# A chunked recurrence scan whose rounds get finer steps, a split product and a kept output bank

## The chip, the cores and the metric

The kernel runs on one NeuronCore of a Trainium2 chip. The metric is the device time of one execution in microseconds (us). The engines are TensorE (PE; its weight loads are PEld), VectorE (DVE), ScalarE (ACT), GpSimd (POOL) and SyncE (SP), each with an in-order queue of its own; they meet only through semaphores.

## The reference, cut to what matters

The reference is two transformer blocks on 256 tokens and 256 context tokens. The change touches one part of the second block, the RWKV scan of its first layer: for 8 heads of 64 and two directions, a state S of 64x64 is carried over 512 tokens.

```python
def step(S, inp):
    r_t, w_t, k_t, v_t, a_t, b_t = inp
    sa = jnp.einsum('bhij,bhj->bhi', S, a_t)
    S = (S * w_t[:, :, None, :] + sa[..., None] * b_t[:, :, None, :]
         + v_t[..., None] * k_t[:, :, None, :])
    return S, jnp.einsum('bhij,bhj->bhi', S, r_t)
s_fin, ys = lax.scan(step, state0, xs, reverse=reverse)
```

## The kernel before, in words

**Units.** The 512 tokens are cut into 4 chunks of 128. A unit is one chunk of one direction d and one pair of heads j (two heads fill the 128 partitions): 4 steps x 4 pairs x 2 directions = 32 units (`self.todo`), numbered n. The eight units of one step are independent of each other; unit n continues the state of unit n-8. The units use four sets of buffers in turn (`self.sets`, NS = 4), so unit n takes over the tiles of unit n-4.

**What a unit does.** ACT makes exponentials of the cumulated decay (EB, EI, three single columns in sm). DVE makes from them RA (two 128x128 parts) and KB (two parts, KB0 and KB1), and scales the state ("ts"). PE multiplies each part of KB with RA, for each of the two heads hh: this is the "four matrices' product" mm, 128x512 for each head, in two PSUM banks. DVE copies it through a triangular mask into MM (`copy_predicated`, two copies of 128x512), which POOL has set to zero before (`memset` of 128x1024). PE transposes KB (kbt), ACT copies that to KBt. ACT copies the diagonal blocks of MM to MC.

Then I plus the strict triangle is inverted in seven levels, i = 0 to 6, of block size 1, 2, ... 64. For level i, POOL makes ML_i, the product of MC with that level's mask (i = 0 to 5; "ml"). PE makes lev_i from ML_i and the factors XX, ACT copies it to T1 ("t"), PE makes xx_i from T1 and XX, and DVE adds it to the factors ("x"; x5 goes to XF in three operations, x6 is one copy). ML is one tile, so ML_1 waits until XX's start has read ML_0; XX shares its tile with KB, so XX's start waits for the transposes. The last level uses XF and MM.

wu0 (PE, 6 records in the trace: state and MM times RA and v) is copied by ACT to WU0; wu1 (PE) gives u, which ACT copies to WU1. st (PE) is KBt times u and KBt times v; y (PE) is state times RA, and MM times u and v. DVE copies or adds y to the output tile and adds st to the state. y of unit n-4 frees the buffers for unit n.

**Order.** The order on every engine is written out by hand. `run` goes through rounds r = 0 to 178; a unit starts every five rounds (APART = 5), and in each round every running unit, oldest first, executes its code up to the next `yield`. So unit n is at its own round r-5n, and four units run at the same time. On PE a unit's own rounds are: 3 mm and kbt, 5 lev0, 6 lev1, 7 xx1, 8 lev2, ... 15 xx5, 16 lev6 and wu0, 17 xx6, 18 wu1, 19 st and y. On POOL: 1 the memset, 3+2i the product ML_i. At the end of a round `close` (steps of the output norm of head pairs 0 to 3, from rounds 146, 159, 165 and 175 on) and `beside` (the output projection of the attention, f = 5, 6, 7 in rounds 0, 2, 4, the bonus term in rounds 4 to 14, the router in round 149) are put in.

**Banks.** `Banks.take` hands out the eight PSUM banks in turn; a taker waits for the tokens of the one before in that bank, which `done` has set.

Helper lines in the profile: L144 matmul, L147 transpose, L150 ACT activation, L153 tensor_tensor, L158 tensor_scalar, L161 scalar_tensor_tensor, L164 tensor_copy, L173 copy_predicated, L179 memset. A matmul has two records in the trace ("x8" is four matmuls). Names: the tiles of set 0 lie in `rwa`; MC and ML lie in rwWU, KB in rwXX, EI in rwT, T1 of set 3 in nv; ps is a PSUM bank.

Of the kernel before, what the change touches and what calls it, by code (L numbers as in the profile page):

```python
# [9 lines left out]
U32 = mybir.dt.uint32  # L10
# [2423 lines left out]
class Rwkv:  # L2434
# [112 lines left out]
    def pe(self, e, beside, amid):  # L2547
# [29 lines left out]
        S.meet(e, p, "prep")  # L2577
        self.run(e, self.unit_pe, self.close_pe, amid)
        S.meet(e, p)
# [93 lines left out]

    def run(self, e, unit, close=None, beside=None):


        running, closing = [], []
        for r in range(self.CLOSE[-1] + 4):
# [6 lines left out]
            assert len(running) <= self.NS  # L2685
# [5 lines left out]
            if beside is not None:  # L2691
                beside(e, r)

# [87 lines left out]
    def unit_pe(self, e, n, step, d, j, B):  # L2781
# [6 lines left out]
        yield  # L2788
        yield
        yield  # L2790
        got = []
        for hh in range(2):
            got.append(g.banks.take(("mm", n, hh)))
            for tok in g.banks.free(("mm", n, hh)):
                e.wait_ge(*tok)
        e.wait_ge(*S.dve.at(("kb", n)))
        for q in range(2):
            for hh, b in enumerate(both):
                ins = e.matmul(got[hh][:, q * 256:(q + 1) * 256], KB[b, q, :], RA[b, :], True, True)
                if q:  # L2800
                    ins.then_inc(*p.up(("mm", n, hh)))
        ps = g.banks.take(("kbt", n))
        for tok in g.banks.free(("kbt", n)):
            e.wait_ge(*tok)
        for q in range(2):
            ins = e.transpose(ps[:, q * P:(q + 1) * P], KB[:, q, :], g.C("ident"))
        ins.then_inc(*p.up(("kbt", n)))
        yield
        for i, li in self.levels():
            yield  # L2810
# [16 lines left out]
            if li == 0:  # L2827
                self.wu0_pe(e, n, RA, MM, state, v)
            if i:
                yield  # L2830
# [16 lines left out]
        yield  # L2847
# [8 lines left out]
        yield  # L2856
        u = WU[:, 1, :]
        e.wait_ge(*S.act.at(("wu1", n)))
        if step < 3:
            ps = g.banks.take(("st", n))  # L2860
            for tok in g.banks.free(("st", n)):
                e.wait_ge(*tok)
            e.wait_ge(*S.act.at(("kbt", n)))
            e.matmul(ps[:, 0:P], KBt[:, 0, :], u, True, False)
            e.matmul(ps[:, 0:P], KBt[:, 1, :], v, False, True).then_inc(*p.up(("st", n)))
        ps = g.banks.take(("y", n))
        for tok in g.banks.free(("y", n)):
            e.wait_ge(*tok)
        e.matmul(ps[:, 0:P], state, RA[:, P:2 * P], True, False)
        for hh, b in enumerate(both):  # L2870
            e.matmul(ps[b, 0:P], u[:, b], MM[:, hh, 128:256], False, False)
        for hh, b in enumerate(both):
            ins = e.matmul(ps[b, 0:P], v[:, b], MM[:, hh, 384:512], False, True)
        ins.then_inc(*p.up(("y", n)))

    def wu0_pe(self, e, n, RA, MM, state, v):
# [4 lines left out]
        e.wait_ge(*S.dve.at(("ts", n)))  # L2881
        e.matmul(ps[:, 0:P], RA[:, 0:P], state, True, False)
# [4 lines left out]
    def unit_act(self, e, n, step, d, j, B):  # L2887
# [7 lines left out]
        yield  # L2895
        if n >= self.NS:
            e.wait_ge(*S.pe.at(("y", n - self.NS)))
            e.wait_ge(*S.dve.at(("end", n - self.NS)))
        e.activation(sm[:, 0:1], mc, ACT.Copy, scale=self.DECAY).then_inc(*a.up())
        e.activation(sm[:, 2:3], mc, ACT.Copy, scale=-self.DECAY).then_inc(*a.up())  # L2900
        e.wait_ge(*a.now())
        e.activation(EB[:, e0:e0 + P], cu, ACT.Exp, scale=-self.DECAY, bias=sm[:, 0:1]).then_inc(*a.up())
        e.activation(EI[:, :], cu, ACT.Exp, scale=self.DECAY, bias=sm[:, 2:3]).then_inc(*a.up())
        e.activation(sm[:, 1:2], mc, ACT.Exp, scale=-self.DECAY).then_inc(*a.up())
        x0 = 0 if d == 0 else 128
        e.activation(EB[:, x0:x0 + 1], mc, ACT.Exp, scale=self.DECAY).then_inc(*a.up(("eb", n)))
        yield
        yield
        e.wait_ge(*S.dve.at(("mk", n)))
        for b in (slice(0, 64), slice(64, 128)):  # L2910
            e.activation(B["MC"][b, :, :], B["MM"][b, :, b], ACT.Copy).then_inc(*a.up(("mc", n)))
        e.wait_ge(*S.pe.at(("kbt", n)))
        e.activation(KBt[:, :, :], two(g.banks.of(("kbt", n))[:, 0:256]), ACT.Copy).then_inc(*a.up(("kbt", n)))
        g.banks.done(("kbt", n), a.now())
        yield
        for i, li in self.levels():
            yield
            if i:
                e.wait_ge(*S.pe.at(("t", n, i)))
                rows = slice(0, P) if li else dst  # L2920
                e.activation(T1[rows, :, :], two(g.banks.of(("lev", n, i))[rows, 0:128]), ACT.Copy).then_inc(*a.up(("t", n, i)))
                g.banks.done(("lev", n, i), a.now())
                if li == 0:
                    e.wait_ge(*S.pe.at(("wu0", n)))
                    e.activation(WU[:, 0, :], g.banks.of(("wu0", n))[:, 0:P], ACT.Copy).then_inc(*a.up(("wu0", n)))
                    g.banks.done(("wu0", n), a.now())
                yield
        yield
# [3 lines left out]
        yield  # L2932

    def unit_dve(self, e, n, step, d, j, B):
# [7 lines left out]
        yield  # L2942
        yield
# [5 lines left out]
        e.tensor_tensor(KB[:, 0, :], self.BB[d][:, j, cc], EI[:, :], MUL).then_inc(*v.up())  # L2949
        e.tensor_tensor(KB[:, 1, :], self.KD[d][:, j, cc], EI[:, :], MUL).then_inc(*v.up(("kb", n)))  # L2950
        e.wait_ge(*v.now())
        e.tensor_scalar(state, state, sm[:, 1:2], None, MUL).then_inc(*v.up(("ts", n)))
        yield
        mask = mid(g.C(f"tri{d}").bitcast(U32), 2, 256)
        for hh in range(2):
            e.wait_ge(*S.pe.at(("mm", n, hh)))
            e.wait_ge(*S.pool.at(("mz", n)))
            e.copy_predicated(two(MM[:, hh, :]), mask, two(g.banks.of(("mm", n, hh))[:, :])).then_inc(*v.up(("mk", n)))
            g.banks.done(("mm", n, hh), v.now())
        yield  # L2960
        for i, li in self.levels():
            yield
            if i == 0:
                one = mid(self.IC[:, :], 2, 64)
                e.wait_ge(*S.pool.at(("ml", n, 0)))
                e.wait_ge(*S.act.at(("kbt", n)))
                e.tensor_tensor(XX[:, 1, :, :], ML[:, :, :], one, ADD).then_inc(*v.up())
                e.wait_ge(*S.pe.at(("t", n, 0)))
                e.tensor_tensor(XX[:, 0, :, :], two(g.banks.of(("lev", n, 0))[:, 0:128]), one, ADD).then_inc(*v.up(("x", n, 0)))
                g.banks.done(("lev", n, 0), v.now())  # L2970
            else:
                yield
                ps = g.banks.of(("xx", n, i))
                e.wait_ge(*S.pe.at(("x", n, i)))
                e.wait_ge(*v.at(("x", n, i - 1)))
                if li > 1:
                    xx = XX[:, :, :, :].rearrange("p q h n -> p (q h n)")
                    e.tensor_tensor(xx, xx, ps[:, 0:256], ADD).then_inc(*v.up(("x", n, i)))
                elif li:
                    x0 = XX[:, 0, :, :].rearrange("p h n -> p (h n)")  # L2980
                    e.tensor_tensor(x0, x0, ps[:, 0:128], ADD).then_inc(*v.up())
                    e.wait_ge(*S.pool.at("compact"))
                    for b in (slice(0, 64), slice(64, 128)):
                        e.tensor_tensor(XF[b, :, b], XX[b, 1, :, :], two(ps[b, 128:256]), ADD).then_inc(*v.up(("x", n, i)))
                else:
                    e.tensor_copy(XF[src, :, dst], two(ps[src, 0:128])).then_inc(*v.up(("x", n, i)))
                g.banks.done(("xx", n, i), v.now())
        yield
        yield
# [8 lines left out]
        if step < 3:  # L2998
            last = e0 + (P - 1 if d == 0 else 0)
            e.wait_ge(*S.pe.at(("st", n)))  # L3000
            e.wait_ge(*v.at(("ts", n)))
            for lo in (0, 64):
                q = slice(lo, lo + 64)
                e.tensor_tensor(state[q, q], state[q, q], g.banks.of(("st", n))[q, q], ADD).then_inc(*v.up())
            g.banks.done(("st", n), v.now())
            e.wait_ge(*v.now())
            e.tensor_scalar(state, state, EB[:, last:last + 1], None, MUL).then_inc(*v.up())
        v.note(("end", n))

    def unit_pool(self, e, n, step, d, j, B):  # L3010
        g, o, S = self.g, self.S.pool, self.S
# [1257 lines left out]
```

## Time and profile before

| what | value |
|---|---|
| median of 3 runs | 2538.28 us (2536.87 to 2542.72) |
| the profiled execution | 2542.52 us, its span 2540.7 us |
| PE busy | 2341.8 us, 92% |
| DVE, ACT, POOL busy | 69%, 41%, 13% |
| one unit of the scan in the steady part | 10.1 us |

The span is the time between the first and the last instruction in the profile; the execution has some us around it. In the table of busy time the groups that cost most belong to other stages; the scan lies between about 1405 and 1757 us. In the rows of the timeline, a line gives start, duration, engine, line, operation, the tiles written and read, shapes and count, and in brackets the idle time of this engine before it and who ended that.

### The profile page before, as it was taken

How to read it: one execution, taken by the hardware profiler on the slowest of the kernel's cores; microseconds unless marked ns; L12 is line 12 of the kernel's file. 1: busy time of each engine (PE TensorE's matmuls, PEld its weight loads, DVE VectorE, ACT ScalarE, POOL GpSimd, SP SyncE). 2: the span in 40 equal slices, each digit the busy share in tenths (PEclk: the TensorE clock that was granted, in tenths of full speed). 3: DMA queues.
4: the chain of work that ended last, by engine and by line, in shares of the span. 5: the costliest groups of instructions: out<-in, count | busy, mean ns of one | idle time of the engine just before them, and what ended most of it. 6: DMA issues, size and time to landing. Idle time of an engine off the chain costs nothing.

```text
span 2540.7 us, 38727 instructions
## 1 busy us (share of the span) xinstructions
PE 2341.8 (92%) x15014; PEld 1751.2 (69%) x15014; DVE 1744.4 (69%) x3348; ACT 1051.7 (41%) x2068; POOL 337.2 (13%) x534
## 2 busy tenths in 40 slices
PE   7999999799989799989999899989999998998997
PEld 3788887465788799944454677775676775667775
DVE  4875687677756687834758666665678885748995
ACT  4222212224231434423134344442477773446884
POOL 0111110010001011000200233331011210001210
PEclk9999999899999899989998999999899999999998
DMA  8566654242226478711111000000389982126995
GB/s 307 190 204 199 216 197 161 94 141 91 101 74 206 142 265 269 254 43 66 39 43 35 18 3 3 2 3 26 109 286 341 324 314 108 59 70 216 338 339 188
DMA packets 114919, 386.47 MB, mean 152 GB/s; under 512 B 20144, under 2 KB 22320, under 8 KB 114480
## 3 DMA queue, kind: packets, MB, share of 16 engines
q1 hardware_dynamic: 76496, 275.81, 31.2%
q0 software_dynamic: 34848, 95.47, 11.3%
q10 hardware_dynamic: 3392, 12.72, 1.3%
q8 instruction: 119, 1.95, 0.3%
q14 instruction: 64, 0.52, 0.1%
HBM read 389.16 MB, written 26.21 MB: 163 GB/s over the span
## 4 chain that ended last, share of the span: by engine, by line
PE 37%; DVE 13%; DMA 8%; ACT 5%; issue 3%; POOL 0%; DVEq 0%; ACTq 0%; SPq 0%; POOLq 0%
PE ps L144 35%; DMA RG<-in_w 5%; DVE moe0wl L153 2%; PE ps L147 2%; DVE moe1wl L153 2%; DMA AR<-in_a 2%; DVE rwMM L173 1%; DVE f2wl L153 1%; DVE acc L161 1%; ACT moe0wh L150 1%; DVE H L161 1%; ACT moe1wh L150 1%; DVE rwXF L153 1%; ACT rwWU L150 1%; DVE rwXX L153 0%
## 5 line engine op out<-in xcount | busy, mean ns | idle before, releaser
L144 PE MATMUL ps<-H,RG 128*128 128x256 f32 (+2 forms) x1088 | 359.4, 491 | 14.0 <-ACT H L150 14.0
L161 DVE SCALAR_TENSOR_TENSOR acc<-AR,cs,acc 128x512 f32<-128x512 f32 x420 | 295.5, 746 | 48.9 <-DMA AR<-in_a 46.7
L144 PEld LDWEIGHTS ps<-H,RG 128*128 128x128 f32 (+1 forms) x1088 | 206.1, 194 | 149.8 <-issue 132.5
L153 DVE TENSOR_TENSOR moe0wl<-RG,moe0wh 128x1024 fp32r<-128x1024 f32 x144 | 173.6, 1219 | 42.8 <-ACT moe0wh L150 33.1
L150 ACT ACTIVATE moe0wh<-RG 128x1024 fp32r<-128x1024 f32 x144 | 150.8, 1061 | 73.9 <-DMA RG<-in_w 44.5
L200 POOL DMA_DIRECT2D AR<-in_a x152 | 82.1, 540 | 698.8 <-DVE acc L161 512.5
L150 ACT ACTIVATE f1wh<-RG 128x1024 fp32r<-128x1024 f32 x66 | 69.7, 1060 | 230.0 <-PE ps L144 229.9
L153 DVE TENSOR_TENSOR moe1wl<-RG,moe1wh 128x1024 fp32r<-128x1024 f32 x120 | 144.2, 1219 | 23.9 <-ACT moe1wh L150 19.8
L144 PE MATMUL ps<-f1hh,f1wh 128*128 128x512 f32 x352 | 142.5, 405 | 4.8 <-DVE f1hl L153 4.8
L150 ACT ACTIVATE moe1wh<-RG 128x1024 fp32r<-128x1024 f32 x120 | 125.9, 1060 | 46.8 <-DMA RG<-in_w 28.4
L144 PE MATMUL ps<-f1hl,f1wh 128*128 128x512 f32 x352 | 140.8, 400 | 0.0
L144 PE MATMUL ps<-f1hh,f1wl 128*128 128x512 f32 x352 | 140.7, 400 | 0.0
L153 DVE TENSOR_TENSOR f1wl<-RG,f1wh 128x1024 fp32r<-128x1024 f32 x66 | 80.4, 1221 | 54.8 <-ACT f1wh L150 53.1
L144 PE MATMUL ps<-f2hh,f2wh 128*128 128x256 f32 x352 | 103.2, 293 | 9.7 <-DVE f2hl L153 5.0
L144 PE MATMUL ps<-f2hh,f2wl 128*128 128x256 f32 x352 | 101.5, 288 | 0.0
L144 PE MATMUL ps<-f2hl,f2wh 128*128 128x256 f32 x352 | 101.4, 288 | 0.0
L150 ACT ACTIVATE f2wh<-RG 128x1024 fp32r<-128x1024 f32 x66 | 68.5, 1055 | 47.9 <-PE ps L144 47.9
L144 PE MATMUL ps<-moe0wh,moe0xh 128*128 128x512 f32 x184 | 78.6, 427 | 9.4 <-DVE moe0wl L153 9.3
L153 DVE TENSOR_TENSOR rwXX<-rwXX,ps 128x256 f32<-128x256 f32 (+1 forms) x120 | 47.1, 393 | 58.1 <-PE ps L144 57.5
L144 PE MATMUL ps<-rwa 64*64 64x64 f32 (+3 forms) x1228 | 74.5, 236 | 12.1 <-DVE rwa L153 5.6
L153 DVE TENSOR_TENSOR f2wl<-RG,f2wh 128x1024 fp32r<-128x1024 f32 x66 | 80.3, 1219 | 7.8 <-ACT f2wh L150 7.7
L144 PEld LDWEIGHTS ps<-f1hh,f1wh 128*128 128x128 f32 x352 | 68.6, 195 | 20.4 <-DVE f1hl L153 6.2
(633 smaller groups left out, 5742.3 us busy)
## 6 DMA issues: line engine op xcount, KB each, us to landing
RG<-in_w SPq DMA_DIRECT2D x524, 512.0 KB
AR<-in_a POOLq DMA_DIRECT2D x152, 512.0 KB, 3.9
moe0back<-moe_outs ACTq DMA_DIRECT2D x4, 1024.0 KB, 8.0
CT<-in_consts ACTq DMA_DIRECT2D x1, 2562.0 KB, 14.9
X<-in_x ACTq DMA_DIRECT2D x1, 2048.0 KB, 11.5
moe_rows<-moe0ht POOLq DMA_DIRECT2D x4, 512.0 KB, 5.4
moe1back<-moe_outs ACTq DMA_DIRECT2D x2, 1024.0 KB, 5.8
X<-in_ctx ACTq DMA_DIRECT2D x1, 1024.0 KB, 5.8
```

The lines of the kernel that those rows point to most:

```text
L144: return Silent() if self.e is None else self.e.matmul(out, lhs, rhs, start=start, stop=stop, skip_group_check=True)
L147: return Silent() if self.e is None else self.e.transpose(out, x, ident)
L150: return Silent() if self.e is None else self.e.activation(out, x, f, **k)
L153: return Silent() if self.e is None else self.e.tensor_tensor(out, a, b, op)
L161: return Silent() if self.e is None else self.e.scalar_tensor_tensor(out=out, in0=a, scalar=s, in1=b, op0=op0, op1=op1)
L173: return Silent() if self.e is None else self.e.copy_predicated(out, mask, data)
L200: return Silent() if self.e is None else self.e.dma_start(out, src)
```

## The change

- `run` passes over the running units four times in a round (`SLOTS = 4`, slots 0 to 3), and each unit's code says for every piece in which of its rounds and which slot it stands (`to(r, slot)`); within a slot the oldest unit is first.
- mm is made and masked in halves. PE multiplies KB0 with RA in the unit's round 2, slot 2, and KB1 with RA in round 3, slot 2, each into a bank per head of which 256 columns are used (four banks per unit in place of two); DVE masks them at 3.0 and 4.2 in four copies of 128x256. RA and KB0 are made at 2.1, KB1 at 3.0.
- The transposes move from behind mm to behind lev0 (5.2), ACT's copy of them to 5.2.
- wu0 stands before lev6 (16.0 and 16.1) instead of behind it.
- y and the state's product share PSUM bank 7, which is kept for them; the other seven turn. State times RA, and KBt times v, come at 17.3, before wu1 (18.0); the parts with u, and MM times v, at 19.2.
- DVE updates the state at 20.0 and takes y at 21.0 (step 3, which has no update: y at 20.0).
- ACT makes the columns and EI at 0.0, waiting for xx6 and ts of unit n-4, and EB at 1.0, waiting for the end of unit n-4.
- POOL's memset of MM goes to 0.0 (it waits for y of unit n-4, as before), ML_0 to 4.1, ML_i to (4+2i).1.

The core of the diff:

```diff
-        b = self.n % len(self.tiles)
-        self.n += 1
+        b = self.n % self.turning if kept is None else kept
+        self.n += kept is None
...
+        g.banks.turning = 7
         self.run(e, self.unit_pe, self.close_pe, amid)
+        g.banks.turning = 8
...
-            for u in list(running):
-                if next(u, "over") == "over":
-                    running.remove(u)
+            for _ in range(self.SLOTS):
+                for u in list(running):
+                    if next(u, "over") == "over":
+                        running.remove(u)
...
+    def clock(self):
+        at = [0]
+        def to(r, slot):
+            for _ in range(r * self.SLOTS + slot - at[0]):
+                at[0] += 1
+                yield
+        return to
...
# unit_pe
+        yield from to(2, 2)
+        self.mm_pe(e, n, 0, KB, RA)
+        yield from to(3, 2)
+        self.mm_pe(e, n, 1, KB, RA)
         for i, li in self.levels():
+            r = 4 + 2 * i if i else 5
+            if i == 6:
+                yield from to(r, 0)
+                self.wu0_pe(e, n, RA, MM, state, v)
+            yield from to(r, 1)
...
+            if i == 0:
+                yield from to(r, 2)
+                ps = g.banks.take(("kbt", n))
...
+            else:
+                yield from to(r + 1, 1)
                 key = ("xx", n, i)
...
+        yield from to(17, 3)
+        out = g.banks.take(("y", n), 7)
...
+        e.matmul(out[:, 0:P], state, RA[:, P:2 * P], True, False)
+        if step < 3:
+            e.wait_ge(*S.act.at(("kbt", n)))
+            e.matmul(out[:, P:2 * P], KBt[:, 1, :], v, False, False)
+        yield from to(18, 0)
         ps = g.banks.take(("wu1", n))
...
+        yield from to(19, 2)
...
+            e.matmul(out[:, P:2 * P], KBt[:, 0, :], u, False, True).then_inc(*p.up(("st", n)))
...
+    def mm_pe(self, e, n, q, KB, RA):
+        g, p, S = self.g, self.S.pe, self.S
+        got = []
+        for hh in range(2):
+            got.append(g.banks.take(("mm", n, q, hh)))
+            for tok in g.banks.free(("mm", n, q, hh)):
                 e.wait_ge(*tok)
+        e.wait_ge(*S.dve.at(("kb", n, q)))
+        for hh, b in enumerate((slice(0, 64), slice(64, 128))):
+            e.matmul(got[hh][:, 0:256], KB[b, q, :], RA[b, :], True, True).then_inc(*p.up(("mm", n, q, hh)))
...
# unit_dve
+        def masks(q):
+            for hh in range(2):
+                e.wait_ge(*S.pe.at(("mm", n, q, hh)))
+                e.wait_ge(*S.pool.at(("mz", n)))
+                e.copy_predicated(MM[:, hh, q * 256:(q + 1) * 256], mask,
+                                  g.banks.of(("mm", n, q, hh))[:, 0:256]).then_inc(*v.up(("mk", n, q)))
...
# unit_pool
-        yield
+        to = self.clock()
+        yield from to(0, 0)
         if n >= self.NS:
             e.wait_ge(*S.pe.at(("y", n - self.NS)))
         e.memset(MM[:, :, :], 0.0).then_inc(*o.up(("mz", n)))
-        yield
         for i, li in self.levels()[:-1]:
-            yield
+            yield from to(4 + 2 * i if i else 4, 1)
             if i:
-                yield
                 e.wait_ge(*S.pe.at(("t", n, i - 1)))
                 e.wait_ge(*S.dve.at(("x", n, 0)))
```

## Rows read from the trace of the kernel before

**Rows 1.** The page, busy time by engine.
```profile
span 2540.7 us, 38727 instructions
...
PE 2341.8 (92%) x15014; PEld 1751.2 (69%) x15014; DVE 1744.4 (69%) x3348; ACT 1051.7 (41%) x2068; POOL 337.2 (13%) x534
```

**Rows 2.** The chain of waits over the scan: start, length, what.
```profile
1439.37 0.71 PE ps L144 x16
...
1568.25 1.34 DVE rwa L173 x2
...
1692.24 0.71 PE ps L144 x16
```

**Rows 3.** Timeline of PE over one period: lev6 to the next xx5.
```profile
1562.35 0.44 PE L144 MATMUL ps<-rwXX,rwMM 64*64 64x64 f32 x4 [0.36 <-DVE rwXF L153]
1562.72 0.49 PE L144 MATMUL ps<-rwst,rwRA 128*128 128x128 f32 x2
...
1563.54 0.45 PE L144 MATMUL ps<-rwXX,rwT 64*64 64x64 f32 x8
...
1564.74 0.45 PE L144 MATMUL ps<-rwXX,rwWU 64*64 64x64 f32 x8 [0.24 <-DVE rwXX L153]
...
1565.59 0.66 PE L144 MATMUL ps<-rwWU,rwXF 128*128 128x64 f32 x4
1566.22 0.45 PE L144 MATMUL ps<-rwXX,rwT 64*64 64x64 f32 x8
...
1567.06 1.13 PE L144 MATMUL ps<-rwa 64*128 64x256 f32 x8
1568.13 0.44 PE L147 MATMUL ps<-CT,rwa 128*128 128x128 f32 x2
...
1569.43 0.39 PE L144 MATMUL ps<-rwMM,rwvk 128*64 128x128 f32 x4
1569.75 0.45 PE L144 MATMUL ps<-rwXX,rwWU 64*64 64x64 f32 x8
...
1570.88 0.45 PE L144 MATMUL ps<-rwXX,rwT 64*64 64x64 f32 x8 [0.21 <-ACT rwT L150]
```

**Rows 4.** Timeline of POOL in that period.
```profile
1563.89 0.95 POOL L179 MEMSET rwa<- 128x1024 f32 x1
1564.80 0.46 POOL L153 TENSOR_TENSOR rwWU<-rwWU,nv 128x128 f32<-128x128 f32 x1
1565.28 0.46 POOL L153 TENSOR_TENSOR rwWU<-rwWU,rwa 128x128 f32<-128x128 f32 x1
```

**Rows 5.** Timeline of DVE: the copy of x6.
```profile
1564.72 0.29 DVE L164 COPY rwXF<-ps 64x128 f32<-64x128 f32 x1
```

**Rows 6.** Timelines of DVE and POOL, 1414 to 1419 us.
```profile
1414.96 0.75 DVE L161 SCALAR_TENSOR_TENSOR rwk<-rwk,VT,abr 128x512 f32<-128x512 f32 x1
...
1418.36 0.94 DVE L161 SCALAR_TENSOR_TENSOR rwk<-rwk,VT,abr 128x512 f32<-128x512 f32 x1
...
1418.30 0.45 POOL L153 TENSOR_TENSOR rwWU<-rwWU,nv 128x128 f32<-128x128 f32 x1 [5.74 <-ACT rwWU L150]
1418.71 0.90 POOL L153 TENSOR_TENSOR rwa<-rwa 128x128 f32<-128x128 f32 x1
```

**Rows 7.** Timelines of DVE and PE at the scan's start.
```profile
1401.23 0.88 DVE L161 SCALAR_TENSOR_TENSOR X<-ps,AC,X 128x256 f32<-128x256 f32 x2 [5.99 <-PE ps L144]
...
1402.22 0.28 DVE L153 TENSOR_TENSOR rwa<-abr,rwa 128x128 f32<-128x128 f32 x1
1402.42 0.29 DVE L153 TENSOR_TENSOR rwa<-rwbb,rwa 128x128 f32<-128x128 f32 x1
...
1419.76 0.45 PE L144 MATMUL ps<-rwa 64*64 64x64 f32 x8 [2.00 <-POOL rwa L153]
...
1429.28 0.68 PE L144 MATMUL ps<-rwa 64*64 64x64 f32 x16 [1.55 <-ACT rwa L150]
```

**Rows 8.** Timeline of PE near the scan's end.
```profile
1727.41 0.45 PE L144 MATMUL ps<-rwXX,rwT 64*64 64x64 f32 x8
...
1749.31 0.52 PE L144 MATMUL ps<-rwXX,rwMM 64*64 64x64 f32 x4 [1.33 <-DVE rwXF L153]
```

More of the change, by code:

```diff
@@ L2826, in unit_pe @@
             ins.then_inc(*p.up(("t", n, i)))
[L2827 to L2830, printed above, removed]
+            if i == 0:
+                yield from to(r, 2)
+                ps = g.banks.take(("kbt", n))
+                for tok in g.banks.free(("kbt", n)):
+                    e.wait_ge(*tok)
+                for q in range(2):
+                    ins = e.transpose(ps[:, q * P:(q + 1) * P], KB[:, q, :], g.C("ident"))
+                ins.then_inc(*p.up(("kbt", n)))
+            else:
+                yield from to(r + 1, 1)
                 key = ("xx", n, i)
@@ L2859, in unit_pe @@
         if step < 3:
[L2860 to L2874 removed]
+            e.matmul(out[:, P:2 * P], KBt[:, 0, :], u, False, True).then_inc(*p.up(("st", n)))
+        for hh, b in enumerate(both):
+            e.matmul(out[b, 0:P], u[:, b], MM[:, hh, 128:256], False, False)
+        for hh, b in enumerate(both):
+            ins = e.matmul(out[b, 0:P], v[:, b], MM[:, hh, 384:512], False, True)
+        ins.then_inc(*p.up(("y", n)))
+    def mm_pe(self, e, n, q, KB, RA):
[4 more added lines that the diff above has]
+            for tok in g.banks.free(("mm", n, q, hh)):
+                e.wait_ge(*tok)
+        e.wait_ge(*S.dve.at(("kb", n, q)))
+        for hh, b in enumerate((slice(0, 64), slice(64, 128))):
+            e.matmul(got[hh][:, 0:256], KB[b, q, :], RA[b, :], True, True).then_inc(*p.up(("mm", n, q, hh)))
     def wu0_pe(self, e, n, RA, MM, state, v):
@@ L2914, in unit_act @@
         g.banks.done(("kbt", n), a.now())
[L2915 to L2928, printed above, removed]
+        for i, li in self.levels()[1:]:
+            yield from to(4 + 2 * i, 1)
+            e.wait_ge(*S.pe.at(("t", n, i)))
+            rows = slice(0, P) if li else dst
+            e.activation(T1[rows, :, :], two(g.banks.of(("lev", n, i))[rows, 0:128]), ACT.Copy).then_inc(*a.up(("t", n, i)))
+            g.banks.done(("lev", n, i), a.now())
+            if li == 0:
+                e.wait_ge(*S.pe.at(("wu0", n)))
+                e.activation(WU[:, 0, :], g.banks.of(("wu0", n))[:, 0:P], ACT.Copy).then_inc(*a.up(("wu0", n)))
+                g.banks.done(("wu0", n), a.now())
+        yield from to(18, 0)
         e.wait_ge(*S.pe.at(("wu1", n)))
@@ L2941, in unit_dve @@
         two = lambda ap: ap.rearrange("p (h n) -> p h n", h=2)
-        yield
-        yield
+        mask = g.C(f"tri{d}").bitcast(U32)
+        to = self.clock()
+        def masks(q):
[4 more added lines that the diff above has]
+                                  g.banks.of(("mm", n, q, hh))[:, 0:256]).then_inc(*v.up(("mk", n, q)))
+                g.banks.done(("mm", n, q, hh), v.now())
+        yield from to(2, 1)
         if n >= self.NS:
@@ new lines, in unit_dve @@
+        yield from to(20, 0)
+        if step < 3:
+            last = e0 + (P - 1 if d == 0 else 0)
+            e.wait_ge(*S.pe.at(("st", n)))
+            e.wait_ge(*S.pe.at(("y", n)))
+            e.wait_ge(*v.at(("ts", n)))
+            for lo in (0, 64):
+                q = slice(lo, lo + 64)
+                e.tensor_tensor(state[q, q], state[q, q], g.banks.of(("y", n))[q, P + lo:P + lo + 64], ADD).then_inc(*v.up())
+            e.wait_ge(*v.now())
+            e.tensor_scalar(state, state, EB[:, last:last + 1], None, MUL).then_inc(*v.up())
+            v.note(("end", n))
+            yield from to(21, 0)
@@ L2997, in unit_dve @@
         g.banks.done(("y", n), v.now())
[L2998 to L3008, printed above, removed]
+        if step == 3:
+            v.note(("end", n))
     def unit_pool(self, e, n, step, d, j, B):
```

129 lines of the change are left out of this document (52 added, 77 removed).

## The prediction

> **What bounds the kernel now.** I read the page first: TensorE (PE) is busy 92% of the span [rows 1], but busy time of pipelined matmuls is no proof of a limit, so I went to the chain of waits over the scan. There the same pieces come back once per unit: the first is at 1439.37 us, the last at 1692.24, 25 units later [rows 2], so a unit takes 252.87/25 = 10.115 us. The timeline of one such period [rows 3] shows what PE does in it. The reader is to see two things: from the start of one group to that of the next is the price of a group (its printed duration overlaps the next one's), and only three rows carry a bracket of idle time. They are a wait for ScalarE's copy of T1 (before 1570.88; ScalarE is late since both 128x512 mask copies and two copies stand ahead of it, rows 2's 1.34 us), one for the factors XF before the last level (1562.35), and one for the factors XX (1564.74).
>
> Prices from [rows 3], in PE time: lev6 0.37 before a wide matmul (I take 0.3 before 64-wide ones), wu0 0.82, xx3 to lev4 1.20 (with its wait; the work in it, 20 records and four that run beside them, is 0.85), lev4 and xx1 0.85, wu1 0.63, xx4 and lev2 (24 records) 0.84, the matrices' product mm 1.07, transposes with st and y 1.62 (transposes 0.27, the rest 1.35), lev5 and xx2, again 24 records, 0.84; xx5, lev3 and lev0, 32 records, 0.84 x 32/24 = 1.12. Without waits that is 0.37+0.82+0.85+0.85+0.63+0.84+1.07+1.62+0.84+1.12 = 9.01. The waits are therefore 1.1 us of a period: 0.35 for XX, 0.75 for the other two.
>
> **The change, part by part.** The work on PE stays the same, matmul for matmul; what changes is order and what is waited for.
>
> Mask copies in four halves: a VectorE (DVE) pair of 128x256 takes 0.88 [rows 7] and the pair of 128x512 mask copies 1.34 [rows 2]. Two pairs of halves are thus at most 1.76, and 1.4 if, as in a pair, each costs its share less the overlap of 0.1; between 0 and 0.4 more DVE time. I take 0.1, off the path: the first pair ends while PE is at wu1 and xx4; the second is wanted by wu0, twelve rounds on, and queued behind it on DVE are the state's update and x5, which so end about 1.8 us after xx5 could start, where lev6 (below) wants x5 after 3.3. EB's exp on ScalarE now waits for that update and is wanted a round later. As the first pair now runs before the level copies and the second after them, ScalarE no longer stands behind it when xx5 wants T1: that wait goes. Putting wu0 (0.82) ahead of lev6 covers the wait for XF: that goes too. The wait for XX stays: between xx3 and lev4 stands the same work (lev1, xx6). Sum so far: -0.75.
>
> The product's first half now comes right behind xx1, 0.85 after lev4. It needs KB0. DVE does, after x3 of lev4's unit, the copy XF (0.02 ahead of lev4), then RA, RA, KB0 at 0.2 each: KB0 starts at +0.60 and ends at +0.88, and PE starts 0.06 later (the start of XF [rows 5], the pitch of 0.20 and the length of 0.28 [rows 7]; 0.06 as an estimate from the 0.14 that PE needs after the slower POOL, below, halved). That is a new wait of 0.09.
>
> GpSimd (POOL) is what decides. The memset of MM moves from round 1 of a unit to round 0, pass 0; it waits for y of unit n-4, which PE finishes in the round just before. The mask product ML3 of unit n-2 stands at round 10, pass 1: the same round, behind it on the in-order queue. Before, ML3 stood ahead of the memset, with two other products between them, so y's end could not hold it. PE wants lev3 right behind xx5 and waits for ML3. Worked out: y ends 0.07 after the next group could start (1569.43+0.39 against 1569.75 [rows 3]); POOL picks up about 0.09 later (estimate from ML5, which starts at 1565.28, behind lev4, 1564.74+0.45 [rows 3, 4]); memset 0.91 from start to start; ML3 0.45 [rows 4]; PE 0.14 after that (1418.71+0.90 against 1419.76 [rows 6, 7]). So lev3 starts 0.07+0.09+0.91+0.45+0.14 = 1.66 us after xx5 could, where 0.54 of xx5 (two thirds of 24 records, rows 3) would do: a wait of 1.12 us in each period. The other waits queued behind it (T3, the transposes, XX's start, ML1) move with lev3; the nearest, ML1 for lev1, ends within 0.1 of when lev1 is wanted, and lev4's own wait hides that.
>
> The new period, once round: 1.66 to lev3, lev3 and lev0 0.57, transposes 0.27, wu0 0.82, lev6 0.3, xx3 to lev4 1.20, lev4 and xx1 with the wait 0.94, first product half 0.54, the parts without u 0.5, wu1 0.63, xx4 and lev2 0.84, second half 0.54, lev5 and xx2 0.84, the parts with u 0.85. Sum 10.50; with lev6 at 0.2 it is 10.40. I take 10.45: +0.33 against 10.115. Units 24 to 31 have no state product (0.45 less PE time); before, the mask chain set the period anyway, now PE and POOL do, so there the period falls to 10.0.
>
> Banks: seven turn instead of eight, 20 takes per unit. I went through the 20: each bank's reader (x5, T3, the start of XX, the KBt copy, WU0, T6, ...) is done at least 0.5 us before the take seven later. Nothing. The kept bank is emptied a round before it is taken.
>
> Start: the product's first half of unit 0 now stands before the output projection of round 2, and its factor comes late: DVE's X update at 1401.23 starts when the projection before is done, KB0 starts at 1402.42 [rows 7]. PE loses about 1402.42+0.28+0.06-1401.05 = 1.7 us. Then it gains: waits of 2.00 (POOL, behind the masks) and 1.55 (ScalarE, behind the masks) [rows 7] mostly go, and the last period before the gate saves 0.8. That is +1.7 less 1.8 and 1.5 and 0.8, and about 1.4 for the shorter waits between them (estimate, from the first product half standing a round earlier): -3.8 us by round 20, where one period's start is 1439.37 [rows 2]; between -2.4 and -5.
>
> Gated periods: 23 by +0.33 = +7.6; rounds 135 to 145, 2 by -0.12 = -0.2; rounds 145 to 160 took 1692.24 to 1727.41 [rows 2, 8], 35.2 us, with three closing matmul pairs and their waits in them; new 3 x 10.0, three pairs of about 1.06 (the 128x512 pairs take what the product's eight records do [rows 3]) and one wait for a bank of 0.7, 33.9: -1.3. End, ungated: 1.33 before lev6 of the last unit [rows 8] is filled by wu0, y's first part fills 0.5 of a wait for XF, and two periods lose the two waits of 0.75: -1.3-0.5-1.5 = -3.3.
>
> Sum without collisions: -3.8+7.6-0.2-1.3-3.3 = -1.0 us.
>
> Collisions of POOL and DVE: ML5 starts 0.54 after lev4, KB0 on DVE at +0.60, both read two tiles of SBUF. The trace shows what such a meeting costs: a DVE operation that took 0.75 alone took 0.94 when it began 0.06 behind a POOL product, and the POOL product after it took 0.90 where 0.45 is usual [rows 4, 6]. So DVE's loss is between 0 (POOL is the one to wait) and about 0.25, on the path to the first product half: 0 to +7 us for 28 periods. RA is in flight when ML5 comes, so either can lose; I take 0.1 each: +2.8.
>
> The Trainium skill ("SBUF — State Buffer", Who interferes with whom) says that a VectorE instruction with two SBUF inputs contends with a GpSimd one that reads SBUF, not with one that only writes, and that the second fully blocks until the first is done. By that rule and rows 6 each side can lose, though DVE lost 0.19 there and not the product's whole 0.45. With the rule's full block the sum would be about +10, by the row's size +3 to +5; the memset, which only writes, would disturb nobody.
>
> Total -1.0+2.8 = about +2 us. The profiled execution took 2542.5 (span 2540.7 [rows 1] and 1.8 around it), which would become 2544.5; it is 4.2 above the median of the runs, 2538.3, so I forecast the median at **2540**.
>
> **Rivals.** (1) Slower: the gate binds and KB0 waits for the whole of POOL's product, 0.45-0.06 = 0.39 [rows 4] in 28 periods, 11 us on top of -1.0: 2548. It decides from 0.22 us per period on (then it is over +5 us). For it: start times 0.06 apart in every period. Against: DVE's three operations are queued back to back. (2) The gate is shorter and the ends give more: 0.15 less per period (POOL ready sooner behind y) is -4, and another 4 at start and end, where PE waits longest: 2538-1-4-4 = 2529. (3) The gate doesn't bind, as PE is late for lev3 for another reason or POOL is faster than its rows: without it the scan saves 1.12 x 28 = 31 more: 2506. Against: the product after the memset starts at 1564.80, 0.91 behind it [rows 4], while its own inputs, lev1's end among them, were there earlier; so the memset is as long as it is drawn. That one of the waits said to go stays (T1's or XF's) is no rival of its own: a wait for T1 before xx5 would only eat into the gate behind it, and XF's would find x5 done long before.
>
> **Numbers.** Forecast 0.50 (its own range 2534 to 2546), rival 1 0.22, rival 2 0.14, rival 3 0.08, and 0.06 for a slower case that I don't see, such as a bank that is not free. The measurement tells 0.2% (5 us) from no change. Faster by more than that: rival 3's 0.08, 0.11 of rival 2 and 0.04 of the forecast's low end, 0.23. Slower: 0.16 of rival 1, the 0.06, and 0.06 of the forecast's high end, 0.28. Same: 0.49. The range for 8 in 10: 2528 to 2551, which takes in rivals 1 and 2 and leaves rival 3 out.
>
> **What would show it.** After the change: PE's idle time before lev3 (64x64 matmuls from the ML tile) with POOL's product as releaser, about 1.1 us once per period, between rounds 20 and 155; POOL's memset starting at y's end in each period, ML3 right behind it; no PE wait for ScalarE's T1 and none for XF before lev6; a period of 10.4 to 10.6 and 10.0 near the end; a wait of 0.1 to 0.3 for KB0 before the first product half; mask copies 56% as long each and twice as many. A period near 9.4 would make the prediction wrong (no gate), one over 10.7 as well (port or banks).

## The result, and the profile after

The changed kernel took 2566.58 us (median of 4 runs, 2562.09 to 2571.75) against 2540.5 for the kernel before on the same chip: ratio 1.0104, 95% interval 1.008 to 1.0129. It is 26 us slower, where 2540 was forecast; the value lies above the range. The profiled execution took 2566.19.

The page, which answers to [rows 1]:

```profile
span 2564.0 us, 38832 instructions
...
PE 2343.4 (91%) x15014; PEld 1743.8 (68%) x15014; DVE 1761.6 (69%) x3412; ACT 1055.0 (41%) x2068; POOL 344.3 (13%) x534
```

PE's work is unchanged: 1.6 us more busy time in a span 23 us longer. The loss is idle time. The chain of waits shows where, beside [rows 2]:

```profile
1568.68 0.95 POOL rwa L179
...
1570.19 0.68 PE ps L144 x16
...
1573.87 0.68 DVE rwa L153 x2
...
1574.59 5.09 PE ps L144 x74
...
1579.73 0.95 POOL rwMM L179
```

Two pieces that the chain before did not have stand in every unit: the memset on POOL, and RA and KB0 on DVE ahead of the product's first half. From one memset to the next is a unit: 1579.73 - 1568.68 = 11.05, on average 11.03, where 10.115 was before and 10.45 forecast. The timeline of PE over that unit, beside [rows 3], wait in brackets:

```profile
1568.53 0.45 PE L144 MATMUL ps<-rwXX,rwT 64*64 64x64 f32 x8
...
1570.19 0.45 PE L144 MATMUL ps<-rwXX,rwWU 64*64 64x64 f32 x8 [0.98 <-POOL rwWU L153]
...
1571.79 0.27 PE L144 MATMUL ps<-rwXX,rwMM 64*64 64x64 f32 x1
...
1572.71 0.27 PE L144 MATMUL ps<-rwXX,rwWU 64*64 64x64 f32 x2 [0.23 <-POOL rwWU L153]
1573.12 0.45 PE L144 MATMUL ps<-rwXX,rwWU 64*64 64x64 f32 x8
...
1574.59 0.70 PE L144 MATMUL ps<-rwa 64*128 64x256 f32 x4 [0.39 <-DVE rwa L153]
```

These are, in order, xx5, lev3, lev6, lev1, lev4 and the product's first half. The three waits, 1.60 us together, are all the idle time that the unit's timeline prints; before it was 0.36 + 0.24 + 0.21 = 0.81 [rows 3]. xx5 and lev6 carry none: the waits for T1 and XF of [rows 3] are gone. lev4 carries none either. The timelines of DVE and of POOL say what the last two waits are made of:

```profile
1573.25 0.29 DVE L164 COPY rwXF<-ps 64x128 f32<-64x128 f32 x1 [0.30 <-PE ps L144]
1573.58 0.29 DVE L161 SCALAR_TENSOR_TENSOR rwa<-rwkk,rwa 128x128 f32<-128x128 f32 x1
1573.79 0.55 DVE L153 TENSOR_TENSOR rwa<-abr,rwa 128x128 f32<-128x128 f32 x1
1574.25 0.28 DVE L153 TENSOR_TENSOR rwa<-rwbb,rwa 128x128 f32<-128x128 f32 x1
```

```profile
1568.68 0.95 POOL L179 MEMSET rwa<- 128x1024 f32 x1 [1.17 <-PE ps L144]
1569.59 0.46 POOL L153 TENSOR_TENSOR rwWU<-rwWU,rwa 128x128 f32<-128x128 f32 x1
1572.11 0.46 POOL L153 TENSOR_TENSOR rwWU<-rwWU,nv 128x128 f32<-128x128 f32 x1 [2.06 <-DVE rwXX L153]
...
1573.65 0.53 POOL L153 TENSOR_TENSOR rwWU<-rwWU,rwa 128x128 f32<-128x128 f32 x1
```

The reader is to see ML3 (1569.59) directly behind the memset, and RA's second operation (1573.79) 0.55 long instead of 0.28, beside ML5 (1573.65), which took 0.53 instead of 0.46.

To compare whole scans free of what lies ahead of them, I take one distance in each profile, "the scan" below: from DVE's X update at the start of the scan (the row of 1401.23 in [rows 7]) to PE's last pair of 128x512 matmuls out of `rwk`, those of the last output norm. Before: 1757.03 - 1401.23 = 355.80. After: 1775.72 - 1395.04 = 380.68, so it is 24.9 longer. The two profiled spans differ by 23.3: the whole loss is in the scan.

### The profile page after: what moved, and what is told of

The parts are those of the page before. It is cut to its first block, busy times and chain, and to the rows that moved or that the text cites. A ratio compares the mean times of both kernels' runs of the same rounds, so it can differ in the third digit from the quotient of the medians.

```text
span 2564.0 us, 38832 instructions
## 1 busy us (share of the span) xinstructions
PE 2343.4 (91%) x15014; PEld 1743.8 (68%) x15014; DVE 1761.6 (69%) x3412; ACT 1055.0 (41%) x2068; POOL 344.3 (13%) x534
## 4 chain that ended last, share of the span: by engine, by line
PE 37%; DVE 13%; DMA 7%; ACT 4%; issue 3%; POOL 2%; DVEq 0%; ACTq 0%; POOLq 0%; SPq 0%
PE ps L144 34%; DMA RG<-in_w 5%; PE ps L147 2%; DVE moe0wl L153 2%; DVE moe1wl L153 2%; DMA AR<-in_a 1%; DVE f2wl L153 1%; DVE acc L161 1%; DVE rwXX L153 1%; POOL rwWU L153 1%; POOL rwMM L179 1%; ACT moe0wh L150 1%; DVE H L161 1%; ACT moe1wh L150 1%; DVE rwa L153 0%
## 5 line engine op out<-in xcount | busy, mean ns | idle before, releaser
L153 DVE TENSOR_TENSOR moe1wl<-RG,moe1wh 128x1024 fp32r<-128x1024 f32 x120 | 144.4, 1219 | 24.8 <-ACT moe1wh L150 20.1
```

What stands on the lines that cost most here:

```text
L153: return Silent() if self.e is None else self.e.tensor_tensor(out, a, b, op)
```

## Experiments

Each ratio is against the kernel before on the same chip, whose median was 2537 to 2538 in the three sets of experiments and 2540.5 in the set of the changed kernel. So two times of different sets are compared by their distance to it, or by the scan. "Unit" is the mean distance between memsets in the one profile of each kernel.

| kernel | time, us | ratio, interval | unit | scan |
|---|---|---|---|---|
| before | 2537 to 2541 | | 10.115 | 355.8 |
| after | 2566.6 | 1.0104 [1.008, 1.0129] | 11.03 | 380.7 |
| a_gate | 2539.2 | 1.0015 [0.9996, 1.0033] | 10.26 | 355.9 |
| b_port | 2554.9 | 1.0074 [1.0052, 1.0096] | 10.72 | 370.9 |
| c_ra | 2550.5 | 1.0058 [1.0039, 1.0077] | 10.60 | 364.1 |
| d_kbt | 2561.6 | 1.0091 [1.006, 1.0122] | 10.86 | 373.6 |
| e_amid | 2563.9 | 1.0115 [1.008, 1.0151] | 11.03 | 379.0 |
| j_gate_mask | 2538.8 | 1.0008 [0.9991, 1.0025] | 10.26 | 356.0 |
| f_all | 2541.3 | 1.0016 [0.9998, 1.0035] | 10.32 | 356.2 |
| i_all_mask | 2537.1 | 1.0002 [0.9983, 1.0021] | 10.32 | 353.0 |
| l_open | 2530.9 | 0.9978 [0.9964, 0.9992] | 9.95 | 345.2 |
| p_ra | 2529.2 | 0.9965 [0.9951, 0.998] | 9.82 | 345.4 |
| n_scale | 2529.1 | 0.9967 [0.9956, 0.9978] | 9.86 | 343.6 |
| q_ra_scale | 2518.1 | 0.9926 [0.9905, 0.9946] | 9.48 | 333.4 |

**a_gate: the memset behind ML3.**

```diff
 def unit_pool(...):
-        yield from to(0, 0)
+        yield from to(0, 2)
```

> The changed kernel with POOL's memset at slot 2 of the unit's round 0 instead of slot 0, so behind ML3 of unit n-2 in place of ahead of it; nothing else. Theory 'gate' (the wait of PE for ML3 is the memset's alone): the wait of 0.97 us before lev3 goes, a period falls from 11.03 by 1.1 to about 9.9, and with 28 such periods the time falls by about 31 us, to 2535. Rival 'it only moves' (x5 on DVE, or the start of XX, is late too and takes over): the wait before lev3 goes, one of 0.5 or more comes before lev6 or lev1, period 10.3 to 10.6, 12 to 20 us less.

The wait before lev3 is gone and the unit 0.77 shorter; the scan is 24.8 shorter, and the time, which was 26 us above the kernel before, is 2 above it. That is the gate, and the largest cost. But 9.9 was expected: part of it moved on, as the rival had it. PE's one longer wait in the unit now is this one, before lev1, beside KB0's, which stays at 0.39:

```profile
1561.38 0.27 PE L144 MATMUL ps<-rwXX,rwWU 64*64 64x64 f32 x2 [0.64 <-DVE rwXX L153]
...
1563.27 0.70 PE L144 MATMUL ps<-rwa 64*128 64x256 f32 x4 [0.39 <-DVE rwa L153]
```

**b_port: two products on POOL held until KB0 is made.**

```diff
                 e.wait_ge(*S.dve.at(("x", n, 0)))
+                if i in (2, 5) and n + i // 2 < len(self.todo):
+                    e.wait_ge(*S.dve.at(("kb", n + i // 2, 0)))
```

> The changed kernel, but POOL's ML2 and ML5 wait until DVE has made KB0 of the unit two or three younger, so that they no longer run beside RA and KB0. Theory 'port' (RA and KB0 are stretched and put off by POOL's products, 0.12 and 0.25 us in a period): RA's second part is back to 0.28 us, KB0 ends 0.35 earlier, the period falls to 10.65 to 10.7, the time by about 10 us, to 2556. Rival 'late chain' (KB0 is late only because x6 before it is): RA's length may fall, the period stays at 11.03 within 0.1.

In the edit the unit whose KB0 is waited for is one or two younger, not two or three. Confirmed: 0.31 per unit. The timeline of DVE, same operation as 1573.79 above:

```profile
1566.90 0.29 DVE L153 TENSOR_TENSOR rwa<-abr,rwa 128x128 f32<-128x128 f32 x1
```

PE no longer waits for KB0.

**c_ra: RA and KB0 ahead of the copy XF on DVE.**

```diff
-        yield from to(2, 1)
+        yield from to(1, 3)
```

> Edit: RA and KB0 stand on VectorE at the end of round 1, ahead of the copy XF of round 2 instead of behind it; nothing else is changed. Theory 'the queue on VectorE': the first product half starts 1.47 us after lev4, where its own work before it takes 0.85, because KB0 stands behind XF, which stands behind lev1's wait, and because RA's second operation shares its time with a product of GpSimd. With RA and KB0 ahead of XF both are gone: no wait before the first product half, period 11.03 - 0.4 to 0.5, so 10.5 to 10.6, and 28 times 0.45 less, about 2554. Rival 'it only moves': RA is then in flight while lev1's product of GpSimd is, or waits for ScalarE's EB, and XF and the start behind it come later; the period stays over 10.9 and the time over 2561.

Confirmed, 0.43 per unit: no wait is left before the first product half, those before lev3 (0.97) and lev1 (0.23) stay. It needs no hold on POOL, since RA then runs before ML5; the operation that meets a product of POOL (at 1563.67) is KB0 (at 1563.71, 0.57 long), early enough not to matter.

**d_kbt: the transposes right behind the second product half.**

```diff
         self.mm_pe(e, n, 1, KB, RA)
+        yield from to(4, 0)
+        ps = g.banks.take(("kbt", n))
...
-                yield from to(r, 2)
-                ps = g.banks.take(("kbt", n))
```

> The changed kernel with the transposes at the unit's round 4, slot 0, ahead of lev0, instead of behind it; the copy of them stays where it is. XX's start on DVE can then run, and free ML0, a group of PE's work earlier. Theory 'late chain' (transposes, XX's start, ML1, lev1, xx6, x6, RA, KB0 in a row set when the first product half can run): the wait for ML1 before lev1 (0.23) and part of that for KB0 (0.39) go, the period falls by 0.25 to 0.3, the time by 7 to 8 us, to 2559. Rival 'port' (KB0's lateness is POOL's products alone): lev1's wait goes but KB0's wait grows by the same, the period falls by under 0.1.

Only in part: lev1's wait is gone in every unit, so XX's start, behind lev0 and the transposes, was what held lev1. But units alternate between 10.66 and 11.06. In the short ones KB0 comes in time, in the long ones PE waits 0.48 for it, and they are no shorter than the 11.03 of the changed kernel, as the rival had it. What parts the two kinds is who loses when RA's second operation meets POOL's ML5. Timelines of DVE and POOL, a short unit and then a long one:

```profile
1564.62 0.28 DVE L153 TENSOR_TENSOR rwRA<-abr,rwEB 128x128 f32<-128x128 f32 x1
1564.69 0.72 POOL L153 TENSOR_TENSOR rwWU<-rwWU,nv 128x128 f32<-128x128 f32 x1 [0.29 <-PE ps L144]
...
1575.36 0.45 POOL L153 TENSOR_TENSOR rwWU<-rwWU,rwa 128x128 f32<-128x128 f32 x1 [0.29 <-PE ps L144]
1575.41 0.55 DVE L153 TENSOR_TENSOR rwa<-abr,rwa 128x128 f32<-128x128 f32 x1
```

Where DVE began first, POOL's product took 0.27 longer and DVE nothing; where POOL began first, by 0.05, it was the other way round. That is the collision of b_port once more, in a kernel that did not touch it. The mean fell by 0.17, and no run says how much of it is lev1's.

**e_amid: the output projections in rounds 0, 1 and 4.**

```diff
-        self.amid = [0, 2, 4]
+        self.amid = [0, 1, 4]
```

> The changed kernel with the attention's output projection f=6 in round 1 instead of 2, so ahead of the first product half of unit 0. Theory (the 1.66 us that PE waits before that half is lost for good): the time falls by 1.6 us, to 2565, and round 20 comes 1.6 earlier behind the projection f=5. Rival (the start is set by unit 0's and 1's own chain of masks, MC, ML0 and by the output's DVE work, so PE's wait there is free): round 20 comes at the same distance within 0.4 us, the time is the same.

The unit is unchanged and the start shorter, as expected; the time, 27 us above the kernel before where the changed one was 26 above it, does not show it. Only a quarter of what the start gained is a wait. The windows from the X update to xx5 of round 20, after and then e_amid (columns: us; busy time of PE, PEld, DVE, ACT, POOL; granted clock; DMA share; GB/s):

```profile
1395.04:1436.13 41.09, 34.18 (x390) 20.58 (x390) 27.25 (x76) 11.86 (x48) 10.33 (x19) 0.96 0.04 14
```

```profile
1402.48:1441.30 38.82, 32.44 (x390) 19.66 (x388) 27.55 (x76) 11.87 (x48) 10.34 (x19) 1.00 0.05 15
```

Of the 2.27, PE's idle time gives 6.91 - 6.38 = 0.53, and its busy time 1.74 for the same 390 records: TensorE's clock. In after the fall lies in two windows of 5 us:

```profile
1405.04:1410.04 5.00, 3.26 (x27) 1.44 (x28) 3.40 (x9) 1.04 (x4) 0.93 (x2) 0.86 0.01 2
1410.04:1415.04 5.00, 4.57 (x50) 2.58 (x47) 3.34 (x8) 1.69 (x7) 0.81 (x2) 0.80 0.01 3
```

That is 5 x (0.14 + 0.20)/0.5 = 3.4 us at 1.2 GHz instead of 2.4, so 1.7 lost. PE had just stood for 1.34 and 0.40 us; a pair of 128x512 matmuls took 1.62 there and 1.12 later on.

**j_gate_mask: a_gate, and the second pair of mask copies ahead of DVE's level copy.**

```diff
-        yield from to(4, 2)
+        yield from to(4, 0)
         masks(1)
```

> Edit: the memset on GpSimd stands behind the mask product of unit n-2 (as in a_gate), and the second pair of mask copies on VectorE stands ahead of the level copy of its round instead of behind it, where VectorE idled 1.09 us. Theory 'VectorE's queue is the second limit': in a_gate the start of XX came 0.64 us late for lev1, behind x5, the state's update and the second mask copies (0.77), all in one stretch without idle time; with the mask copies out of that stretch lev1's wait goes and KB0's 0.39 stays: period 10.26 - 0.64 = 9.6, time about 2539 - 28 x 0.64 = 2521. Rival: the start of XX is held by TensorE or GpSimd (T3's transposes, ML0), then the period stays 10.2 and the time 2539.

My theory falls: unit 10.26, wait 0.64 as before, though the mask copies moved to 1561.71, into idle time. What follows them shows why (timeline of DVE):

```profile
1563.65 0.47 DVE L153 TENSOR_TENSOR rwst<-rwst,ps 64x64 f32<-64x64 f32 x2 [0.66 <-PE ps L144]
1564.16 0.48 DVE L158 TENSOR_SCALAR rwst<-rwst,rwa 128x128 f32<-128x128 f32 x1
1564.67 0.29 DVE L153 TENSOR_TENSOR rwXX<-rwXX,ps 128x128 f32<-128x128 f32 x1
1564.87 0.60 DVE L153 TENSOR_TENSOR rwXF<-rwXX,ps 64x128 f32<-64x128 f32 x2
1565.50 0.29 DVE L153 TENSOR_TENSOR rwXX<-rwWU,rwa 128x128 f32<-128x128 f32 x1
1565.82 0.29 DVE L153 TENSOR_TENSOR rwXX<-ps,rwa 128x128 f32<-128x128 f32 x1
```

DVE idles 0.66 until PE has finished y, and then runs without a break: the state's update, its scaling, x5, the start of XX. The stretch is bound at its front by y, not by what stands ahead of it; lev1 waits for ML1 on POOL, and ML1 for the end of XX's start.

**f_all and i_all_mask: gate, port, amid and kbt together; i with the mask copies as well.**

> Edit: the four repairs together: memset behind the mask product (a_gate), two products of GpSimd wait for KB0 (b_port), the output projections in rounds 0, 1, 4 (e_amid), the transposes of KB right behind the second product half (d_kbt). If the three periodic costs are separate, the period is 10.26 (a_gate) less 0.31 (b_port) less 0 to 0.17 (d_kbt), 9.8 to 9.95, and with 2 us less at the start the time is 2539 - 9 - 2 to -5 = 2523 to 2528. Rival 'they overlap': once the gate is open the wait for KB0 is set by lev1's and XF's lateness, the hold on GpSimd only delays lev4's product, and the time stays within 3 us of a_gate's, 2536 to 2541.

> Edit: f_all with the second pair of mask copies ahead of the level copy of its round on VectorE. Theory 'VectorE's queue is the second limit': no wait of over 0.2 us is left in the period, which is then the work alone and the sharing of it, 9.2 to 9.35; against f_all 0.6 us less in each of 28 periods, about 2509. Rival: the mask copies are not the cause and the time is f_all's.

Both missed: units of 10.32, above a_gate's, with waits of 0.19 before lev6 and 0.55 before lev1. f_all's time (2541.3) is its rival's, i_all_mask's is no better within its interval; its scan is 3.2 shorter, but not in the steady units. With the gate open, transposes moved out of the time in which PE waits for DVE add 0.37 of work to the rest of the unit. That is the theory that the next four tested.

**l_open: f_all without moving the transposes.** (Edits of a_gate, b_port and e_amid.)

> Edit: f_all without moving the transposes: memset behind the mask product, two products of GpSimd wait for KB0, output projections in rounds 0, 1, 4. Theory 'a stretch on VectorE from the end of y': in f_all and i_all_mask VectorE works without a break from the end of the output's parts with u (state's update 0.5, its scaling 0.5, x5 0.8, start of XX 0.6, T3 and x3) for 3.2 us, and TensorE has less than that to do until lev1, so it waits 0.19 and 0.55; the transposes (0.37), moved out of that gap, made it wider. With them back in it the period is 10.32 - 0.37 = 9.95, and against f_all 2541 - 28 x 0.37 = 2531. Rival: the start of XX again waits for the transposes, and the period is a_gate's 10.26 less 0.31 for KB0's wait only if that wait was not hidden; if both just trade places the period stays 10.2 and over.

Unit 9.95, time 2530.9: both as expected. KB0's wait is gone, one of 0.64 before lev1 is all that is left in a unit.

**p_ra: edits of a_gate, e_amid and c_ra. n_scale and q_ra_scale: l_open and p_ra with the state's scaling behind the start of XX.**

```diff
                 e.tensor_tensor(state[q, q], state[q, q], ...)
+            yield from to(20, 2)
             e.wait_ge(*v.now())
             e.tensor_scalar(state, state, EB[:, last:last + 1], None, MUL)
```

> Edit: memset behind the mask product, output projections in rounds 0, 1, 4, and RA and KB0 ahead of the copy XF as in c_ra (no hold on GpSimd). If the stretch on VectorE sets the period, it is that of l_open within 0.1 (9.85 to 10.05), since KB0 is then early in either; about 2531. Rival: XF behind RA delays what waits for it, period over 10.1.

> Edit: l_open with the scaling of the state (0.5 of VectorE's time) behind the start of XX instead of ahead of x5. By the theory of the stretch on VectorE, the start of XX ends 0.5 earlier, the wait before lev1 goes, and the period is l_open's less 0.3 to 0.5: 9.5 to 9.65, about 2520. Rival: ScalarE's EB, which waits for the scaling and stands ahead of T6's copy in its queue, comes 1 us later and TensorE then waits for T6 or for KB0 instead; the period does not fall by more than 0.1.

> Edit: p_ra with the scaling of the state behind the start of XX. By the stretch on VectorE 0.3 to 0.5 less than p_ra, 9.5 to 9.65, about 2520; as RA is wanted earlier here than in n_scale, a late EB would show here first, as a wait before the first product half, and the period would be p_ra's.

p_ra came within 0.13 of l_open's unit, where 0.1 was expected, and on the short side. In n_scale the rival came true: the wait before lev1 fell from 0.64 to 0.26, but one of 0.27 to 0.35 for KB0 came, and the unit falls by 0.09 only. Its path is the rival's: EB waits on ACT for the scaling,

```profile
1566.17 0.40 ACT L150 ACTIVATE rwEB<-H,rwsm 128x128 f32<-128x128 f32 x1 [0.66 <-DVE rwst L158]
```

T6's copy behind it starts 1.06 after lev6, where l_open has 0.47, and xx6, XF, RA and KB0 follow it. With RA ahead of XF (q_ra_scale) KB0's wait is gone and the theory's 9.5 is there, 0.34 below p_ra. No wait for the late EB shows there. Its timeline of DVE has the stretch in the new order, and POOL's has ML1:

```profile
1560.26 0.47 DVE L153 TENSOR_TENSOR rwst<-rwst,ps 64x64 f32<-64x64 f32 x2
1560.80 0.29 DVE L153 TENSOR_TENSOR rwXX<-rwXX,ps 128x128 f32<-128x128 f32 x1
1561.00 0.59 DVE L153 TENSOR_TENSOR rwXF<-rwXX,ps 64x128 f32<-64x128 f32 x2
...
1562.02 0.29 DVE L153 TENSOR_TENSOR rwa<-ps,rwa 128x128 f32<-128x128 f32 x1
1562.35 0.29 DVE L158 TENSOR_SCALAR rwst<-rwst,rwEB 128x128 f32<-128x128 f32 x1
...
1562.87 0.42 DVE L153 TENSOR_TENSOR rwXX<-rwXX,ps 128x256 f32<-128x256 f32 x1
```

```profile
1562.46 0.49 POOL L153 TENSOR_TENSOR rwa<-rwa 128x128 f32<-128x128 f32 x1 [1.29 <-DVE rwa L153]
```

PE's timeline has one wait in a unit:

```profile
1563.09 0.45 PE L144 MATMUL ps<-rwa 64*64 64x64 f32 x8 [0.27 <-DVE rwk L153]
```

This is lev1 again, and what is left of its wait for ML1. The row names another operation of DVE, the one that happened to end last; but ML1 (1562.46) ends 0.14 before lev1 starts, the distance that POOL's product has to lev3 in the changed kernel, and in later units the same wait of 0.26 is printed with POOL as its releaser. x3 (1562.87) ends only after lev1 has started, so it is not waited for here.

This version beats both kernels: 19 us below the one before on its chip (0.9926, 0.9905 to 0.9946), and with the 26 that the changed kernel lies above it, some 45 below the changed one; the scan is 47 shorter.

## Why the prediction was wrong

**The gate** was right in kind and size. lev3 starts 1570.19 - 1568.53 = 1.66 after xx5, the forecast figure; the memset waits for y and ML3 stands behind it in each steady unit; a_gate took it away and gained 0.77 per unit. What I had not priced is what stands behind the gate: opening it did not bring the 1.12 that rival 3 counted with.

**Waits said to go:** T1's and XF's went, as forecast. The wait for XX that was to stay before lev4 is gone too; in its place lev1 waits 0.23 for ML1, whose product waits for XX's start.

**The step that failed in each unit is the wait for KB0 before the product's first half**: 0.94 was forecast from lev4 to it, 1.47 came. KB0 was to start 0.60 after lev4 and started at 1574.25 - 1573.12 = 1.13. The forecast's own three pitches add up to 0.58, so 0.55 is to be explained: 0.15 is the copy XF (0.13 behind lev4 instead of 0.02 ahead; lev4 no longer waits, and xx6 stands behind lev1, which does), 0.13 the larger gap from XF to RA, and 0.26 the pitch from RA's second operation to KB0, 0.46 instead of 0.20, beside ML5. I had written that lev4's own wait hides the lateness of lev1; it hid it for lev4, not for the queue on DVE. Two experiments with different means, b_port and c_ra, remove 0.31 and 0.43. Rival 1 named the collision with POOL's product; it was the one that I should have given more, since the row of 0.94 against 0.75 [rows 6] already showed that DVE can be the one to lose. But the collision is half of the 0.53, and with rival 1's price the sum was 2548: the queue on DVE ahead of RA stood in no rival.

The rest of the unit nearly cancels against the forecast's terms: wu0, lev6 and wu1 were 0.11, 0.29 and 0.14 cheaper, the two product halves 0.09 each, xx3 to lev4 0.12, the transposes with the other small terms 0.10 and the parts with u 0.16 dearer. Over the 23 units this is 23 x (11.03 - 10.45) = 13.3 us; between rounds 20 and 135 the trace has +21.1 where +7.6 was forecast.

**The start** failed next: -3.8 forecast, +2.95 measured from the X update to xx5 of round 20 (41.09 against 38.14). The 1.7 that PE was to lose on KB0 of the first unit came (1.66). But the waits of 2.00 and 1.55 [rows 7] did not go, they moved. PE's idle time in that stretch is 6.91 after and, by the same window of the trace before, 38.14 - 31.16 = 6.98 there. PE's timeline of after:

```profile
1396.66 0.70 PE L144 MATMUL ps<-rwa 64*128 64x256 f32 x4 [1.66 <-DVE rwa L153]
...
1407.36 0.45 PE L144 MATMUL ps<-rwa 64*64 64x64 f32 x8 [1.34 <-POOL rwa L153]
...
1421.33 0.70 PE L144 MATMUL ps<-rwRA,rwXX 64*128 64x256 f32 x4 [0.75 <-DVE rwXX L153]
...
1426.77 0.45 PE L144 MATMUL ps<-rwXX,rwWU 64*64 64x64 f32 x8 [0.67 <-DVE rwa L153]
```

Each product half brought its own wait for KB0 (0.43, 0.75, 0.36 in the three units after the first), and the gate closed a unit earlier than I had it (1426.77 starts 0.15 after ML3 ends, which stood behind a memset; the row names DVE). The rest is busy time, +3.0: 1.7 of clock, as measured on e_amid, and the other 1.3 in part the halves of the product, each 0.09 dearer; that part is only argued.

**The smaller terms:** rounds 135 to 145 +0.55 for -0.2, 145 to 160 +1.4 for -1.3, the end -1.2 for -3.3. The errors add up: 13.5 + 6.75 + 0.75 + 2.7 + 2.1 = 25.8, from -1.0 to +24.8; of these the forecast had 2.8 in its term for collisions. For the last two no run tells the causes apart.

**Why the change, its gate opened, still gains nothing** (a_gate): it takes away the printed waits of before, 0.81 in a unit, and puts 0.64 for lev1 and 0.39 for KB0 in their place, 1.03; the unit is 0.15 longer. The second limit is the stretch on DVE from y's end through the state's update and scaling, x5 and XX's start. l_open (transposes back in PE's gap, -0.37 against f_all) and q_ra_scale (0.5 of DVE's work out of the stretch, -0.34 against p_ra) show it from two sides. In part that 0.5 is POOL's doing: the scaling runs beside the memset there and takes 0.48, where it took 0.29 before and in q_ra_scale (last section). The prediction had the memset disturb nobody; what its 0.19 is worth in a unit no run shows by itself. Starting that stretch at the end of the state's own part, ahead of the output's parts with u, would need that part in a bank of its own; it wasn't tried.

## What to carry to other kernels

When an instruction that waits moves up in an in-order queue, look at what stood ahead of it and now stands behind: here one line, the memset two passes too early, was worth some 24 us. Then ask what the next wait is when that one goes; work that fills an engine's idle time must stay in the gap where the engine idles, and what can leave is the work on the other engine's unbroken stretch. A sum of prices per unit needs each operation's start followed through the queue in which it stands, since a lateness that one engine hides is still there for what is queued behind it on another.

## What the runs showed of the hardware

RA's second operation, a VectorE operation of 128x128 on two SBUF tiles, takes 0.28 to 0.29 alone (before, b_port). It took 0.54 to 0.55 beside a POOL product of the same size that began 0.05 to 0.14 ahead of it (after, the long units of d_kbt); KB0 took 0.57 where the product began 0.04 ahead (c_ra). Where the product began 0.07 behind RA's second operation (the short units of d_kbt), VectorE kept its 0.28, and the product took 0.72 instead of 0.45. In after the product took 0.53 as well: it had itself begun 0.07 behind RA's first operation. So mostly the second one loses. Not always: in q_ra_scale KB0 began 0.01 behind a product and kept its 0.28, and the product, which had begun 0.19 behind RA's second operation, took 0.60.

The Trainium skill ("SBUF — State Buffer", Who interferes with whom) calls the port pair that the two engines share an exclusive lock, and has the order of issue decide who is blocked. d_kbt's two kinds of unit agree with the order. The sizes are smaller than what was left of the other's row: in after RA's second operation lost 0.27 where the product still had 0.39 to go. KB0 in q_ra_scale does not fit it.

The memset, which only writes, kept its 0.95 beside DVE's work in every run, and a VectorE operation of 128x512 on SBUF tiles kept 0.74 beside it (before, at 1410.91), as the same section lets expect of operations with two inputs. But it is not free for all: the state's scaling (`tensor_scalar`, 128x128), which took 0.28 to 0.31 in the kernel before, took 0.48 in all 24 units of after in which the memset ran beside it, and in each run with the scaling in its old place; in n_scale and q_ra_scale, where it no longer meets the memset, it took 0.28 to 0.29. The rows are of after and of before, each directly behind the state's update:

```profile
1569.22 0.48 DVE L158 TENSOR_SCALAR rwst<-rwst,rwa 128x128 f32<-128x128 f32 x1
...
1570.57 0.29 DVE L158 TENSOR_SCALAR rwst<-rwst,rwEB 128x128 f32<-128x128 f32 x1
```

A stop of PE of 1.34 us at the start of the scan had 3.4 us at 1.2 GHz right behind it (after; a_gate, b_port and j_gate_mask alike, with 0.85 to 0.88 and 0.78 to 0.80 in the two windows). c_ra, with the projections in the same rounds and a stop of 1.34, kept 1.00; so did d_kbt with one of 1.08 and e_amid with one of 1.35. What decides between them stays open.
